# A state-space scan whose cumulative sums are taken from high and low parts, with the rows' scaling moved behind the next unit's exponential

## What is computed

```python
xdt = xh * dt[..., None]
adt = dt * a                              # per token and head, the decay's logarithm
a_cs = jnp.cumsum(adt, axis=-1)           # within a chunk
seg = a_cs[..., :, None] - a_cs[..., None, :]
ldec = jnp.exp(jnp.where(causal, seg, -jnp.inf))
cb = jnp.einsum('bclgn,bcsgn->bcgls', cc, bc)
y_diag = jnp.einsum('bcgjls,bcsgjp->bclgjp', cb[:, :, :, None] * ldec, xdt)
decay_states = jnp.exp(a_cs[..., -1:] - a_cs)
states = jnp.einsum('bclgn,bcgjl,bclgjp->bcgjpn', bc, decay_states, xdt)
# over chunks: h = h * exp(a_cs[..., -1]) + states; prev = h before each chunk
y_off = jnp.einsum('bclgn,bcgjpn,bcgjl->bclgjp', cc, prev, jnp.exp(a_cs))
y = y_diag + y_off + d_skip * xh
yz = y * silu(z)
yz = yz * rsqrt(mean(yz * yz, group of 512) + 1e-5)
```

## Time and profile before

| | us |
|---|---|
| median of 3 runs | 2109.1 |
| lowest, highest | 2109.01, 2120.7 |
| the profiled execution | 2109.57 |
| its span, first to last instruction | 2108.3 |
| mean granted TensorE clock | 0.988 |

### The profile page before, as it was taken

The page is one execution under the profiler, slowest core; times in us unless marked ns, Lnnn a source line. Parts: engine busy times, 40 slices in busy tenths (PEclk is TensorE's granted clock), DMA queues, the critical chain, the costliest instruction groups (busy, mean ns, idle before and its releaser), DMA issues.

```text
span 2108.3 us, 24436 instructions
## 1 busy us (share of the span) xinstructions
PE 2022.3 (96%) x9260; PEld 1536.7 (73%) x9260; DVE 1410.3 (67%) x2159; ACT 873.4 (41%) x1524; POOL 653.2 (31%) x484
## 2 busy tenths in 40 slices
PE   8999989999999999899999999999999989999997
PEld 6778856787557676566678787888787667778885
DVE  7668676422346889445517699899998756784649
ACT  5333276333445662344412333444224544362431
POOL 3676520552101112345434000000003544235443
PEclk9999999999999999999999999999999999999999
DMA  6422330442401112311043211121133112556322
GB/s 259 134 58 77 109 118 21 170 140 76 135 20 41 41 51 80 100 41 50 21 170 114 86 42 60 32 79 50 60 110 117 64 55 73 193 190 219 110 81 110
DMA packets 72429, 197.91 MB, mean 94 GB/s; under 512 B 11182, under 2 KB 20559, under 8 KB 71800
## 3 DMA queue, kind: packets, MB, share of 16 engines
q1 hardware_dynamic: 72168, 196.35, 27.2%
q10 hardware_dynamic: 144, 0.00, 0.0%
HBM read 152.89 MB, written 46.71 MB: 95 GB/s over the span
## 4 chain that ended last, share of the span: by engine, by line
PE 60%; DVE 16%; ACT 4%; issue 3%; POOL 2%; DMA 2%; SPq 0%; DVEq 0%; ACTq 0%; POOLq 0%
PE psum L262 57%; DVE m L2878 3%; PE psum L265 3%; POOL m L307 1%; DMA m<-in_w 1%; DVE m L2899 1%; DVE m L2111 1%; PE psum L1984 1%; ACT m L297 1%; DVE m L317 1%; DVE m L536 1%; DVE m L452 1%; DVE m L527 1%; DVE m L3070 1%; DVE m L3051 1%
## 5 line engine op out<-in xcount | busy, mean ns | idle before, releaser
L262 PE MATMUL psum<-m,m 128*128 128x512 f32 (+8 forms) x8420 | 1920.8, 393 | 51.9 <-DVE m L2235 10.6
L262 PEld LDWEIGHTS psum<-m,m 128*128 128x128 f32 (+4 forms) x8420 | 1443.0, 187 | 503.3 <-issue 157.6
L307 POOL TENSOR_TENSOR m<-m,m 128x1024 fp32r<-128x1024 f32 (+1 forms) x122 | 309.0, 2537 | 1023.1 <-ACT m L297 1022.7
L297 ACT ACTIVATE m<-m 128x1024 fp32r<-128x1024 f32 (+2 forms) x166 | 173.6, 1049 | 355.0 <-PE psum L262 222.7
L2878 DVE SCALAR_TENSOR_TENSOR m<-m,m,m 128x1024 f32<-128x1024 f32 x240 | 310.2, 1294 | 6.3
L265 PE MATMUL psum<-m,m 128*128 128x128 f32 x784 | 110.5, 277 | 20.3 <-ACT m L2399 5.7
L265 PEld LDWEIGHTS psum<-m,m 128*128 128x128 f32 x784 | 90.5, 142 | 40.8 <-ACT m L1431 10.6
L2111 DVE TENSOR_SCALAR_CACHE_REDUCE m<-m,m 128x896 bf16<-128x896 f32 (+4 forms) x130 | 102.7, 847 | 1.0
L2235 DVE CUSTOM_DVE_ANT_0 m<-psum,m 128x128 f32<-128x128 f32 (+3 forms) x64 | 48.2, 754 | 55.2 <-POOL m L2436 21.5
L2436 POOL TENSOR_TENSOR m<-m,m 128x384 f32<-128x384 f32 (+5 forms) x48 | 72.2, 1525 | 11.3 <-DVE m L2235 11.3
L2341 ACT ACTIVATE m<-m,m 128x1024 bf16<-128x1024 f32 (+1 forms) x62 | 64.1, 1037 | 23.6 <-DVE m L2138 23.6
(11 more groups left out here) (305 smaller groups left out, 1649.4 us busy)
## 6 DMA issues: line engine op xcount, KB each, us to landing
m<-in_w SPq DMA_DIRECT2D x164, 512.0 KB, 3.5
scr_hscr<-m SPq DMA_DIRECT2D x4, 2048.0 KB, 6.6
m<-scr_hscr SPq DMA_DIRECT2D x4, 2048.0 KB, 10.9
scr_turned<-scr_strip SPq DMA_DIRECT2D x8, 575.5 KB, 12.6
m<-in_x SPq DMA_DIRECT2D x4, 1024.0 KB, 7.8
scr_gscr<-m SPq DMA_DIRECT2D x16, 256.0 KB, 4.1
m<-in_x SPq DMA_DIRECT2D x2, 2048.0 KB, 8.4
m<-scr_turned SPq DMA_DIRECT2D x8, 512.0 KB, 3.5
```

The costliest lines, as they stand in the source:

```text
L262: return self.nc.tensor.matmul(out, lhsT, rhs, start=start, stop=stop, skip_group_check=True)
L297: k.nc.scalar.activation(k.hi[SLOT[i]][:, 0:kk * n], k.raw[i % 2][:, 0:kk * n], ACT.Copy).then_inc(*k.up("w_hi", i))
L307: k.nc.gpsimd.tensor_tensor(lo, raw, hi.bitcast(F32), ALU.subtract).then_inc(*k.up("w_lo", i))
```

## The change

The decays' logarithms AD (line 2539 of the kernel before) get a high part AH in float32r, made by ScalarE, and a low part AL = AD - AH, made by VectorE in the z stage; both lie over constants that are no longer needed. The mask `tgt` is converted in place to float32r (`later`). For each unit ScalarE now makes sixteen scaled copies of the mask, eight from AH (RH) and eight from AL (RL), written in float32r; TensorE makes seg from four matmuls in float32r in place of two in float32. RL lies over a convolution buffer, so the first copies also wait for that buffer's store (`cv_out`, 6). The chunk's small sums stay in float32.

The scaling of the output's rows leaves `post` and becomes `scale`. It is issued for unit u-2 in unit u, behind the exponential of u and the sixteen copies for u+1, from unit 2 on; the last two are issued behind the loop.

```diff
--- before.py
+++ after.py
@@ -182,6 +182,10 @@
         self.tgt = self.tile(o, [128]); o += 512
         self.bones = self.tile(o, [128]); o += 512
         self.flip = self.tile(o, [128]); o += 512
+
+        self.low, self.high = self.tile(o - 1024, [128]), self.tile(o - 512, [128], F32R)
+
+        self.later = self.tile(o - 1536, [128], F32R)
         self.mhalf = self.tile(o, [16]); o += 64
         self.epsc = self.tile(o, [32]); o += 128
         self.tiny = self.tile(o, [256]); o += 1024
@@ -2537,6 +2541,8 @@
         self.BT, self.CT, self.BN = k.tile(Q0, [2, 1024]), k.tile(Q0 + 8 * KB, [2, 1024]), k.tile(Q0 + 16 * KB, [8, 256])
         self.cvr = [k.tile(Q0 + (24 + 4 * i) * KB, [1024]) for i in range(2)]
         self.DT, self.AD = k.tile(PH + 64 * KB, [8, 16]), k.tile(PH + 64 * KB + 512, [8, 16])
+
+        self.AH, self.AL = (x.rearrange("p (b n) -> p b n", b=8) for x in (k.high, k.low))
         self.an = k.tiny[:, 224:240]
         self.x0 = Ring(k, "se_x0", [0, 1, 2, 3], [("h2", 0, b) for b in range(4, 8)])
         self.x1 = Ring(k, "se_x1", [4, 5, 6, 7], [("h2", 1, b) for b in range(4, 8)])
@@ -2549,7 +2555,7 @@
         self.dt = self.XN[0:16, :, 896:1024]
         self.zr = [k.tile(Z0 + 2 * KB * i, [512]) for i in range(6)]
 
-        self.R = k.tile(H0, [8, 128])
+        self.RH, self.RL = k.tile(H0, [8, 128], F32R), k.tile(Q0 + 24 * KB, [8, 128], F32R)
         self.E = [k.tile(H0 + 4 * KB + 4 * KB * i, [8, 128]) for i in range(2)]
         self.XD, self.XE, self.YB = ([k.tile(H0 + (12 + 4 * j + 2 * i) * KB, [8, 64]) for i in range(2)] for j in range(3))
         self.ZS = [k.tile(H0 + 24 * KB + 2 * KB * i, [512]) for i in range(2)]
@@ -2744,7 +2750,8 @@
     def chunk(c):
         bank = k.bank(B.one.take("sum", c))
         pe.wait_ge(*B.one.freed("sum", c))
-        for i, mask in enumerate((k.tle, k.tgt, k.ones)):
+        pe.wait_ge(*at("later"))
+        for i, mask in enumerate((k.tle, k.later.bitcast(F32), k.ones)):
             ins = k.mm(bank[:, 16 * i:16 * i + 16], mask, B.AD[:, c, :], i == 0, i == 2)
         ins.then_inc(*up("sd_sum", c))
 
@@ -2753,9 +2760,9 @@
         pe.wait_ge(*at("sd_R", c, g))
         if (c, g) != (0, 0):
             pe.wait_ge(*at("sd_exp", *before((c, g), 1, 2)))
-        r = B.R.rearrange("p a b -> p (a b)")
         for i in range(2):
-            ins = k.mm(k.bank(2 + i), k.tgt, r[:, 512 * i:512 * i + 512], True, True)
+            for r in (B.RH, B.RL):
+                ins = k.mm(k.bank(2 + i), k.later, r[:, 4 * i:4 * i + 4, :].rearrange("p a b -> p (a b)"), r is B.RH, r is B.RL)
         ins.then_inc(*up("sd_seg", c, g))
         bank = k.bank(B.one.take("cb", c, g))
         pe.wait_ge(*B.one.freed("cb", c, g))
@@ -2938,6 +2945,9 @@
         for i in range(4):
             dve_panel(k, after(f"z{h}{i}"))
             taps(8)
+            if (h, i) == (0, 0):
+                dve.wait_ge(*at("ad_hi"))
+                V.tensor_tensor(B.AL, B.AD, B.AH.bitcast(F32), ALU.subtract).then_inc(*up("ad_lo"))
     taps.room(2)
     k.mark("se_z")
     k.marks(dve, "se_z", ("act", "pool"))
@@ -3196,6 +3206,8 @@
             late.put(5, "dt")
     k.mark("se_in")
     k.marks(act, "se_in", ("pe", "dve"))
+    A.activation(B.AH, B.AD, ACT.Copy).then_inc(*up("ad_hi"))
+    A.activation(k.later, k.tgt, ACT.Copy).then_inc(*up("later"))
     for h in range(2):
         for i in range(3):
             act_panel(k, after(f"z{h}{i}"))
@@ -3222,7 +3234,9 @@
 
     def ahead(c, g):
         for h in range(8):
-            A.activation(B.R[:, h, :], k.tle, ACT.Copy, scale=B.AD[:, c, 8 * g + h:8 * g + h + 1]).then_inc(
+            n = 8 * g + h
+            A.activation(B.RH[:, h, :], k.tle, ACT.Copy, scale=B.AH.bitcast(F32)[:, c, n:n + 1]).then_inc(*up("sd_R", c, g, h, "high"))
+            A.activation(B.RL[:, h, :], k.tle, ACT.Copy, scale=B.AL[:, c, n:n + 1]).then_inc(
                 *up("sd_R", c, g, h, also=[("sd_R", c, g)] if h == 7 else ()))
 
     def pre(c, g):
@@ -3250,6 +3264,10 @@
                 *up("sd_pva", c, g, also=[("sd_pv", c, g), ("free", "se_one", "state", c, g)]))
         act.wait_ge(*at("sd_yz", c, g))
         A.activation(B.ZS[i], B.YB[i].rearrange("p a b -> p (a b)"), ACT.Square, accum_out=k.tiny[:, 240 + 2 * g:241 + 2 * g]).then_inc(*up("sd_sq", c, g))
+
+    def scale(c, g):
+
+        i = (2 * c + g) % 2
         act.wait_ge(*at("sd_rs", c, g))
         A.activation(B.XN[:, c, 512 * g:512 * g + 512], B.YB[i].rearrange("p a b -> p (a b)"), ACT.Copy, scale=k.tiny[:, 240 + 2 * g:241 + 2 * g]).then_inc(
             *up("sd_out", c, g))
@@ -3258,14 +3276,17 @@
     for m, half in B.front:
         cgate(m, half)
         if (m, half) == (0, 1):
-            act.wait_ge(*at("ad"))
+            act.wait_ge(*at("ad_lo"))
             act.wait_ge(*at("cv_tap", 4, 30))
+            act.wait_ge(*at("cv_out", 6))
             ahead(0, 0)
     k.marks(act, "se_z", ("pe", "dve", "pool"))
     for c, g in B.units:
         if g == 0:
             chunk(c)
         pre(c, g)
+        if (c, g) > (0, 1):
+            scale(*before((c, g), 2, 2))
         if (c, g) in B.cgates:
             cgate(*B.cgates[c, g])
         if (c, g) == (7, 1):
@@ -3273,7 +3294,9 @@
         if prev:
             post(*prev)
         prev = (c, g)
+    scale(7, 0)
     post(*prev)
+    scale(*prev)
     k.mark("se_sd")
 
     act_transposes(k, B.one, "ys", k.sm("sng"), (1,))
```

## The result

The changed kernel takes 2125.89 us (median of 11 runs, 2124.39 to 2134.55); the kernel before, timed beside it, 2112.96 us (11 runs, 2109.01 to 2121.18). The ratio is 1.0061, its 95% interval 1.0046 to 1.0075: 12.9 us slower. The forecast, 2122.0 on the median shown of 2109.1, is the same ratio of 1.0061.

What follows compares the result with a forecast made beforehand. A ring of dependences and TensorE's stream were taken to bind the scan in turn. Units +16.1, head -2.4, end -1.3 and low part +0.3 make +12.7 us on 2109.1: 2122 us, range 2102 to 2133 (8 in 10).

Steps and rivals of the forecast that it cites:

- The scaling of the rows: Scan: moved behind the copies, it delays GpSimd's first instruction of a unit to 6.4 us behind the exponential.
- rings: Scan: the chain of dependences from one exponential to the next, through ScalarE, GpSimd and VectorE; 11.51 us without a panel.
- Rings with a panel: Scan units 5, 7, 10, 13: GpSimd's low part of a weight panel adds 2.31 us, making 13.82 us.
- The sum: Whole kernel: units +16.1, scan's head -2.4, end -1.3, low part +0.3, in all +12.7 us.
- head: Scan from unit 0's exponential to unit 4's: 38.9 against 41.3 us, -2.4; called the weakest term.
- end: End of scan: the last gate copy (7,1) follows exponential and scaling, 1.6 us after the last exponential began, -1.3 us.
- The copies: ScalarE, scan: sixteen copies at 0.29 us take 4.66 us, 2.33 more per unit.
- rival D: ScalarE, scan: the copies don't overlap, 1.6 us more in each of eleven units, 2139 us; chance 0.06.
- The matmuls: TensorE, scan: four cheaper products save 0.82 us per unit, 13.1 over 16 units, but this ends as idle time.
- B: TensorE, scan: the matmuls' saving counts in full, -13.1 us, giving 2096 us; chance 0.03.
- A: Scan: the ring doesn't wait for GpSimd's decay; without a panel TensorE or VectorE sets the pace, 2104 us; chance 0.13.
- C: TensorE, scan: its clock falls to half in nearly every unit after longer idle gaps, 2132 us; chance 0.13.

Runs made afterwards that it cites:

- e8: Changed kernel with four output buffers for two, low copies written over the high ones (high part left out of the sum): 2113.4 us, 0.9995 of before.
- e3: Changed kernel with the scaling of unit u-2 between the exponential and the sixteen copies: 2115.3 us, 1.0008 of before.
- e12: Changed kernel with GpSimd making the panel's low part behind the two tiny steps of u-1, not ahead of the decay: 2122.4 us, 1.0035 of before.
- e6: Changed kernel with TensorE's waits filled by 180 matmuls of no use, to keep its clock up: 2132.8 us, 1.0090 of before.
- e4: Changed kernel with the scaling between exponential and copies, and GpSimd's decay ahead of the panel's low part: 2114.1 us, 0.9996 of before.
- e1: Changed kernel with the scaling put back behind its square, sixteen copies and four matmuls kept: 2125.7 us, 1.0054 of before.
- e2: Kernel before with only the scaling moved to its late place, full-precision sums and eight copies kept: 2106.9 us, 0.9961 of before.
- e7: Changed kernel without the low part of the decays' logarithms, so eight copies and two matmuls per unit: 2104.4 us, 0.9959 of before.
- e10: Changed kernel with GpSimd's decay of u-1 moved ahead of the panel's low part: 2124.5 us, 1.0048 of before.
- e5: Kernel before (full precision, eight copies) with the scaling between exponential and copies, and the decay ahead of the panel's low part: 2107.7 us, 0.9968 of before.

## Why the prediction was right

**The scaling of the rows**, its main step, held in each link: D 6.37 us behind the exponential (6.4), rings of 11.47 (11.51), the state sum released by the decay in all eleven units, with 3.45 and 5.31 us in the two above and 4.6 on average, where I had said 2 to 4 in nearly every unit. e8 and e3 show that this wait is the cause. Rings with a panel were 13.83, 13.92, 14.22 and 14.36 for 13.82: in the two longest D or XE ran beside VectorE's L2989 (1.40 for 1.04 above), the overlap that I had kept 1 us for. e12 bears out the panel's term of 2.31 x 4 = 9.2, with 7.8 measured.

**The sum**, term by term, between the profiled executions: units +16.9 (forecast +16.1), head -2.8 (-2.4), end -0.1 (-1.3), start and z stage +0.5 (+0.3), and +1.0 that arose ahead of any changed instruction, with 0.3 behind the scan: 15.8, the difference of the spans (2124.1 and 2108.3). The medians differ by 12.9, forecast 12.7; the nearness is partly luck, since runs of one kernel scatter by more than the 3 us between them. So is the head's: its intervals were 7.01, 9.91, 9.65 and 11.92 us for 7.1, 9.4, 10.8 and 11.6, up to 1.2 off each way.

**Mis-sized** was the end. The gate copy (7,1) doesn't follow exponential and scaling, it still waits for TensorE, which was behind after its last slow stretch:

```profile
1782.68 1.00 ACT L3247 ACTIVATE m<-psum 128x1024 f32<-128x1024 f32 x1
1783.72 0.72 ACT L3272 ACTIVATE m<-m,m 128x512 f32<-128x512 f32 x1
1785.46 0.60 ACT L3255 ACTIVATE m<-psum 128x512 f32<-128x512 f32 x1 [1.02 <-PE psum L266]
```

**The copies** took 4.67 us (4.66); rival D is out. **The matmuls**: some 10 us less work from T(0) to T(15), fifteen units (forecast 13.1 for sixteen), and none of it gained in the eleven units, as forecast; B is out. TensorE's waits in the 180 us came to 23.1 where I had said over 25. **A** is out: the state sum was released by the decay in eleven units, not by TensorE. **C**: the clock did fall behind most waits, as C had it, and e6 shows that this cost nothing between T(4) and T(15), because TensorE had more in hand than it lost; at most the 1.2 us at the end are its. That holds for the changed kernel's long ring, not for e4's short one.

**Wrong, or missed, in the reading of before**: I had TensorE's 10.92 us and more bind a unit, in turn with the ring. It does not bind each unit: four of before's seven intervals without a panel are 9.14 to 9.68 us and two are 10.33, and e1, with 0.82 us less for TensorE, has the same 10.33 and 9.14. The early scaling made the ring late, TensorE waited for copies and caught up in units such as 9 (12.5 us before, 9.66 in e2). Moved alone the scaling wins 5.8 us, and then the ring sets the pace (e2, e7). I had priced the two parts only together, and so missed that one of them was a gain. The forecast didn't need this reading, since the new ring is longer than TensorE's work either way.

## What to carry to other kernels

When an instruction is moved behind others on its engine, look for who overwrites what it reads: here a reader put behind sixteen copies held back, over two buffers, an instruction at the head of another engine's queue and all that stood behind it. Price each part of a change alone and then together, since a gain (e2) can hang on a wait that the other part lengthens. Work taken off an engine is worth nothing while a longer chain sets the pace (e7). A slow clock is free or not by the same test: ask whether anyone waits for the engine.

## What the runs showed of the hardware

The price of one GpSimd instruction of 2.4 us depended on its place: 7.8 us over four panels in the ring, some 5 of them back when it lay beside VectorE's product with z (e10), nothing beside one with time in hand (e12). The product with two operands in SBUF took 2.20 us for 0.68, the state sum, with one in PSUM, its usual 0.69 beside the same instruction. The Trainium skill, SBUF — State Buffer, section "SBUF: two separate sides", gives the whole pair of ports to whichever began first; from the rows, waiting for the low part's end makes 1.65 + 0.68 = 2.33 us for the product (2.20 measured) and 2.35 + 1.23 = 3.58 for that of e12 (3.44), so the trace agrees within 0.15.

TensorE's granted clock in the scan fell behind waits of 1.8 to 5.1 us in most of these kernels, but not behind every such wait: it fell to 0.50 behind 1.81 us in e4 and stayed at 1.00 behind 1.77 in e3, behind 2.11 in e2 and behind 2.28 in e5. In e6, whose waits were filled, it was 1.00 throughout. The Trainium skill, TensorE: Matmul & The Clock Gate, section "HAM oscillation — how this bites in real kernels", has each burst behind idle time start slow; the traces agree behind most waits, not behind those of e2 and e5. e6 adds that a fall is free where no one waits for the engine, and e4's head that it costs where someone does (1.6 us for one).
